# Modulation products on two column groups, second halves inside the recurrent heads, constants behind the first modulation weights

## What is computed

```python
def _modulation(cond, w_ada, b_ada):
    m = jnp.einsum('bd,de->be', jax.nn.silu(cond), w_ada) + b_ada
    return tuple(jnp.split(m[:, None, :], 6, axis=-1))

# in each layer
shift1, scale1, gate1, shift2, scale2, gate2 = mods
h = _rms(x, norm1_w) * (1 + scale1) + shift1
p = h @ w_in          # attention, recurrence (HGRN2, both directions), 2-D DFT, side by side
x = x + gate1 * (mix @ w_out)
h2 = _rms(x, norm2_w) * (1 + scale2) + shift2
x = x + gate2 * moe(h2)    # 4 groups of 4 experts, top-1 group, top-2 expert
```

## Time and profile before

| | |
|---|---|
| median of 3 runs | 1977.4 us (1970.61 to 1978.65) |
| the profiled execution | 1976.31 us; its span from first to last instruction 1974.5 us |
| PE busy, PEld busy | 1718.8 us (87%), 1199.9 us (61%) |
| DVE, ACT, POOL busy | 684.0 us (35%), 432.1 us (22%), 317.5 us (16%) |
| mean granted TensorE clock | 0.929 |
| L1331, modulation products | 768 records, 178.1 us |
| HBM traffic | 279.46 MB read, 34.60 MB written |

### The profile page before, as it was taken

How to read it: one execution, slowest core, us unless ns; L and a number is a source line. 1 busy time by engine, 2 the same in 40 slices (tenths; PEclk the granted TensorE clock), 3 DMA queues, 4 the chain that set the end, 5 groups by cost and what they waited for, 6 DMA issues and landing times.

```text
span 1974.5 us, 24830 instructions
## 1 busy us (share of the span) xinstructions
PE 1718.8 (87%) x10290; PEld 1199.9 (61%) x10290; DVE 684.0 (35%) x1200; ACT 432.1 (22%) x750; POOL 317.5 (16%) x303
## 2 busy tenths in 40 slices
PE   5899998776798999999998989887669968999993
PEld 2345556565654568888844555566565547888873
DVE  1107523577401312122114672356760151212223
ACT  1413232522102210000014313353220121000002
POOL 4000003854100010000010000276320001000001
PEclk9999997978699899999999989898789969999996
DMA  9672111000001489999995211000000038999975
GB/s 326 202 249 65 43 51 37 1 2 2 1 28 58 160 295 356 369 361 368 344 359 188 45 54 51 24 2 2 1 3 0 0 158 291 368 366 365 362 263 170
DMA packets 143495, 315.67 MB, mean 160 GB/s; under 512 B 25024, under 2 KB 99192, under 8 KB 130456
## 3 DMA queue, kind: packets, MB, share of 16 engines
q1 hardware_dynamic: 120240, 241.88, 36.1%
q0 software_dynamic: 11104, 37.26, 5.1%
q10 hardware_dynamic: 12040, 34.95, 4.5%
HBM read 279.46 MB, written 34.60 MB: 159 GB/s over the span
## 4 chain that ended last, share of the span: by engine, by line
PE 77%; DVE 11%; ACT 6%; issue 3%; DMA 2%; SPq 0%; ACTq 0%; POOL 0%; DVEq 0%; POOLq 0%
PE ps L1289 18%; PE ps L1660 18%; PE ps L1674 9%; PE ps L1331 8%; ACT scr L550 4%; PE ps L1401 3%; PE ps L1514 3%; PE ps L1644 2%; PE ps L1424 2%; PE ps L1439 2%; DVE scr L914 2%; PE ps L1318 1%; PE ps L1569 1%; DVE hT L1085 1%; DMA ring<-in_w_ada_dram 1%
## 5 line engine op out<-in xcount | busy, mean ns | idle before, releaser
L1660 PEld LDWEIGHTS ps<-hT,ring 128*128 128x128 f32 x3200 | 366.2, 193 | 26.4 <-issue 22.0
L1660 PE MATMUL ps<-hT,ring 128*128 128x128 f32 x3200 | 367.0, 276 | 3.4 <-ACT hT L550 3.4
L1289 PE MATMUL ps<-hT,ring 128*128 128x512 f32 x960 | 269.6, 442 | 18.2 <-DVE pT L959 12.7
L1289 PEld LDWEIGHTS ps<-hT,ring 128*128 128x128 f32 x960 | 149.7, 195 | 140.4 <-issue 127.1
L1331 PE MATMUL ps<-ring,cond 128*2 128x256 f32 x768 | 178.1, 387 | 11.6 <-DMA ring<-in_w_ada_dram 7.0
L550 ACT ACTIVATE pT<-ps 128x256 f32<-128x256 f32 (+3 forms) x74 | 33.5, 458 | 677.4 <-PE ps L1660 488.3
L1674 PE MATMUL ps<-ring,pT 128*128 128x512 f32 x400 | 179.6, 592 | 0.0
L517 POOL DMA_INDIRECT pT<-h_rows,slot_tok x50 | 47.2, 944 | 796.0 <-PE ps L1644 427.7
L478 POOL TENSOR_SCALAR scr<-scr,st 128x640 f32<-128x640 f32 (+1 forms) x80 | 129.1, 1627 | 73.8 <-DVE st L968 73.8
L1289 PE MATMUL ps<-pT,ring 128*128 128x512 f32 (+1 forms) x512 | 139.0, 434 | 1.7 <-ACT pT L550 1.7
L1249 DVE TENSOR_TENSOR pT<-ps,pT 128x256 f32<-128x256 f32 x50 | 21.2, 424 | 324.5 <-ACT pT L550 324.5
(11 more groups left out here) (212 smaller groups left out, 1961.1 us busy)
## 6 DMA issues: line engine op xcount, KB each, us to landing
ring<-in_w_gate_dram SPq DMA_DIRECT2D x50, 1024.0 KB, 7.4
ring<-in_w_up_dram SPq DMA_DIRECT2D x50, 1024.0 KB, 7.7
ring<-in_w_down_dram SPq DMA_DIRECT2D x50, 1024.0 KB, 6.9
ring<-in_w_ada_dram SPq DMA_DIRECT2D x48, 1024.0 KB, 6.3
y_rows<-pT ACTq DMA_DIRECT2D x50, 512.0 KB, 8.1
ring<-in_w_in_dram SPq DMA_DIRECT2D x14, 1024.0 KB, 5.3
h_rows<-scr ACTq DMA_DIRECT2D x10, 512.0 KB, 2.6
ring<-in_w_in_dram SPq DMA_DIRECT2D x16, 256.0 KB, 4.6
```

The costliest lines, as they stand in the source:

```text
L1289: ins = mm(out[:, a:b], lhs, rhs[:, a:b], start=start, stop=stop, **kw)
L1660: last = mm(bank(2 + j, P, at + c * P), w[:, k, c * P:(c + 1) * P], xk[:, j, k, :], start=(k == 0), stop=(k == KC - 1))
```

## The change

Five things, one after the other:

- A product writes to two column groups: even k to rows 0 to 31 of the bank, odd k to rows 32 to 63, with 32 stationary columns each (`cond` becomes a flat row of 46, so that columns 2k and 2k+1 are the wanted ones and the other 30 are other k's or zeros). ScalarE copies 64 rows, and a matmul with a 64 x 2 selector `sel` adds the two groups and turns the row into columns, in place of the transpose.
- The second half of each layer moves into that layer's recurrent heads: in the two units with d = 0, six items each, one ahead of the diagonal and one behind each of the first five levels. Their rows go to bank 7 beside the output products, one buffer, and their columns to another place of bank 7. The list of weights has them between the projection and the output weights of the layer.
- `norm` on ScalarE is split in `root` and `shift`. In layer 0 PE does the norm sums first, then the 12 items, and ScalarE the root first.
- SP loads only `ident` and `ones` ahead of x. Nine constants follow the issue of the second projection item ("MID"), `dft_s` and `dft_p` the fifth ("LATE"); the waits move to the first users. The cast of `lvl` follows the scaling of layer 0's norm on VectorE, and ScalarE waits for it before its first projection evacuation.
- The combine of layer 0 has no modulation items; `weigh` runs straight on.

```diff
@@ weight_stream
         if l == 0:
-            s += [("ada", l, i) for i in range(2 * ADA_HALF)]
+            s += [("ada", l, i) for i in range(ADA_HALF)]
         s += [("in", l, i) for i in range(IN_ITEMS)]
+        s += [("ada", l, ADA_HALF + i) for i in range(ADA_HALF)]
         s += [("out", l, i) for i in range(OUT_ITEMS)]
         if l + 1 < DEPTH:
             s += [("ada", l + 1, i) for i in range(ADA_HALF)]
         s += expert_items(l)
-        if l + 1 < DEPTH:
-            s += [("ada", l + 1, ADA_HALF + i) for i in range(ADA_HALF)]
@@
-CONSTS = ("ident", "blockones", "ones", "rot", "tri", "dft64", "cosT", "sinT",
-          "dft_s", "dft_p", "lvl", "restart", "tileno")
+CONSTS = ("ident", "ones", "restart", "lvl", "blockones", "rot", "cosT", "sinT", "tri", "dft64", "tileno",
+          "dft_s", "dft_p")
+FIRST_CONSTS, MID_CONSTS, LATE_CONSTS = CONSTS[0:2], CONSTS[2:11], CONSTS[11:]
@@ rows of a product
+        def ada_row(i):
+            return bank(2 + i % 2, 256)
+        def ada_row_next(i):
+            return bank(4 + i % 2, 256)
+        ada_row_heads = bank(7, 256, P)
+        HEADS_MODS = 3 * P
@@ sync
+                if (kind, l, i) == ("in", 0, 1):
+                    for c in MID_CONSTS:
+                        sp.dma_start(lvl_f if c == "lvl" else K[c][:], C[c]).then_inc(consts_in, 16)
+                if (kind, l, i) == ("in", 0, 4):
+                    for c in LATE_CONSTS:
+                        sp.dma_start(K[c][:], C[c]).then_inc(dft_in, 16)
@@ scalar
             act.wait_ge(zero_done, 3)
-            ada(0, 0)
             for l in range(DEPTH):
+                root(l, 0)
+                if l == 0:
+                    for i in range(ADA_HALF):
+                        ada(0, 0, i, ada_row(i))
                 act.wait_ge(mods_ok, 2 * l + 1)
-                norm(l, 0)
+                shift(l, 0)
                 if l == 0:
-                    ada(0, 1)
+                    act.wait_ge(lvl_ok, 1)
@@
                             A_(scr[:, 2 + i % 2, :], scr[:, 2 + i % 2, :], ACT.Exp).then_inc(lv_e, 1)
+                            if d == 0 and i >= 1:
+                                ada(l, 1, 6 * p + i - 1, ada_row_heads)
+                        if d == 0:
+                            ada(l, 1, 6 * p + 5, ada_row_heads)
@@ vector
+            seq(V.memset(cond[:], 0.0))
+            V.tensor_tensor(sel[:], ident[0:64, 0:2], ident[0:64, 32:34], ALU.add)
...
-            dve.wait_ge(consts_in, 16 * N_CONST)
-            seq(V.tensor_copy(K["lvl"][:], lvl_f))
@@
                 norm(l, 0)
                 if l == 0:
-                    modulations(0, 1)
+                    dve.wait_ge(consts_in, 16 * N_CONST)
+                    V.tensor_copy(K["lvl"][:], lvl_f).then_inc(lvl_ok, 1)
@@
+                modulations(l, 1)
                 dve.wait_ge(f_ab, l + 1)
@@ tensor
+            def ada_product(l, half, i, row, evacuated):
+                w = item(ITEM["ada", l, ADA_HALF * half + i]).rearrange("p (k n) -> p k n", k=KC)
+                if evacuated > 0:
+                    pe.wait_ge(ada_sb, evacuated)
+                for k in range(KC):
+                    r = slice(32 * (k % 2), 32 * (k % 2) + 32)
+                    last = mm(row[r, :], cond[:, 2 * k:2 * k + 32], w[:, k, :], start=(k < 2), stop=(k >= KC - 2))
+                last.then_inc(ada_ps, 1)
+            def ada_columns(l, half, i):
+                pe.wait_ge(ada_sb, (2 * l + half) * ADA_HALF + i + 1)
+                for j in range(2):
+                    last = mm(bank(7, 2, HEADS_MODS * half + 4 * i + 2 * j), mrow[:, i % 2, j * P:(j + 1) * P], sel[:],
+                              start=True, stop=True)
+                last.then_inc(ada_tr, 1)
@@
-            ada(0, 0, 0, ADA_HALF)
-            pe.wait_ge(consts_in, 16 * N_CONST)
-            pe.wait_ge(late_in, 16 * 16 * DEPTH)
             for l in range(DEPTH):
                 norm(l, 0)
                 if l == 0:
-                    pe.wait_ge(mods_ok, 1)
-                    pe.wait_ge(nrs, 1)
-                    ada(0, 1, 0, ADA_HALF)
+                    ada(0, ada_row, 0, ADA_HALF)
@@ in the heads, after the state products
+                        def row_product(a):
+                            ada_product(l, 1, 6 * p + a, ada_row_heads, (2 * l + 1) * ADA_HALF + 6 * p + a)
+                        if d == 0:
+                            row_product(0)
@@ in the heads, after each level's scores
                             last.then_inc(g_ps, 1)
+                            if d == 0 and i <= 5:
+                                ada_columns(l, 1, 6 * p + i)
+                                if i < 5:
+                                    row_product(i + 1)
@@ in the combine
-                if l + 1 < DEPTH:
-                    pe.wait_ge(dn_sb, MT * (l + 1))
-                    ada(l + 1, 1, 0, ADA_AT[0])
```

More of the change, by code:

```diff
@@ L377, in _ @@
         def _(sp):
-            sp.dma_start(K["ident"][:], C["ident"]).then_inc(x_in, 16)
+            for n in FIRST_CONSTS:
+                sp.dma_start(K[n][:], C[n]).then_inc(x_in, 16)
             sp.dma_start(xrow[:, 0, :], A["x_prompt"][0]).then_inc(x_in, 16)
             sp.dma_start(xrow[:, 1:TT, :], A["x_sample"][0].rearrange("(t p) d -> p t d", p=P)).then_inc(x_in, 16)
-            for n in CONSTS[1:]:
-                sp.dma_start(lvl_f if n == "lvl" else K[n][:], C[n]).then_inc(consts_in, 16)
             def next_item(n):
@@ L584, in _, with root @@
                     A_(xT[:, :, t * P:(t + 1) * P], ps[:, 0:1024].rearrange("p (k t) -> p k t", k=KC), ACT.Copy).then_inc(xt_act, 1)
-            def norm(l, which):
+            def root(l, which):
                 n0 = (l * 2 + which) * KC
@@ L600, in norm, with shift @@
                 A_(rs, rs, ACT.Exp, scale=-0.5).then_inc(nrs, 1)
+            def shift(l, which):
+                n0 = (l * 2 + which) * KC
                 for k in range(KC):
@@ L605, in norm, with ada @@
                            bias=mods[:, l, 3 * which, k, g:g + 1]).then_inc(h_ok, 1)
[L607 to L614, removed]
+            def ada(l, half, i, row):
+                n = (2 * l + half) * ADA_HALF + i
+                act.wait_ge(ada_ps, n + 1)
+                if n >= 2:
+                    act.wait_ge(ada_tr, n - 1)
+                A_(mrow[:, i % 2, :], row[0:64, :], ACT.Copy).then_inc(ada_sb, 1)
             def evacuated(l, u):
@@ L739, in _ @@
                     A_(pT[:, C_FT + p, 0:NP], bank(7, NP), ACT.Copy).then_inc(f_os, 1)
-                norm(l, 1)
+                root(l, 1)
+                shift(l, 1)
                 act.wait_ge(lgt_ps, l + 1)
@@ L756, in _ @@
                 if l + 1 < DEPTH:
-                    ada(l + 1, 0, 0, 5)
+                    for i in range(5):
+                        ada(l + 1, 0, i, ada_row_next(i))
                 act.wait_ge(rt_m, 2 * l + 1)
@@ L762, in _ @@
                 if l + 1 < DEPTH:
-                    ada(l + 1, 0, 5)
+                    for i in range(5, ADA_HALF):
+                        ada(l + 1, 0, i, ada_row_next(i))
                 def half_x(i):
@@ L882, in modulations @@
                 seq(V.tensor_tensor(mods[:, l, 3 * half:3 * half + 3].rearrange("p s k g -> p (s k) g"),
-                                    bank(7, 48).rearrange("p (n g) -> p n g", g=2), bias, ALU.add))
+                                    bank(7, 48, HEADS_MODS * half).rearrange("p (n g) -> p n g", g=2), bias, ALU.add))
                 at = (PA_N1, PA_N2)[half] + 8 * l
@@ L1271, in _ @@
                                                ALU.mult, ALU.add).then_inc(x_new, 1)
-                if l + 1 < DEPTH:
-                    modulations(l + 1, 1)
         @block.tensor
@@ L1319, in norm, with ada @@
                     mm(bank(6, NP), ones[:], sq[:, 0:NP], start=(k == 0), stop=(k == KC - 1)).then_inc(nsum, 1)
-            def ada(l, half, first, end):
+            def ada_product(l, half, i, row, evacuated):
[12 more added lines that the diff above has]
+                last.then_inc(ada_tr, 1)
+            def ada(l, row, first, end):
                 for i in range(first, end + (end == ADA_HALF)):
-                    n = (2 * l + half) * ADA_HALF + i
                     if i < ADA_HALF:
-                        w = item(ITEM["ada", l, ADA_HALF * half + i]).rearrange("p (k n) -> p k n", k=KC)
-                        if n >= 2:
-                            pe.wait_ge(ada_sb, n - 1)
-                        for k in range(KC):
-                            last = mm(bank(4 + i % 2, 256)[0:2, :], cond[:, :, k], w[:, k, :], start=(k == 0), stop=(k == KC - 1))
-                        last.then_inc(ada_ps, 1)
-                    if i >= 1:
-                        pe.wait_ge(ada_sb, n)
-                        for j in range(2):
-                            last = nc.tensor.transpose(bank(7, 2, 4 * (i - 1) + 2 * j), mrow[:, (i - 1) % 2, j * P:(j + 1) * P],
```

(5 more changed lines are left out.)

38 lines of the change are left out of this document (17 added, 21 removed).

## The result

The changed kernel takes 1919.8 us (1919.5 to 1921.4), the kernel before 1977.3 (1970.6 to 1978.7). The ratio is 0.9717, with a 95% interval of 0.9695 to 0.974: 57.5 us faster, where 54.5 were forecast. The profiled execution took 1921.4 us, with a span of 1919.6.

What follows compares the result with a forecast made beforehand. It took TensorE's program order to bound the first 138 us. Gains of 72.5 (start), 13 (routing) and 9 (combine) less 40 (heads) gave 54.5 us: 1976.3 to 1921.8, stated as a median of 1923 us, range 1900 to 1950.

Steps and rivals of the forecast that it cites:

- The product: Modulation product on two column groups: 1.9 us in place of 3.55, with a 0.45 us merge 2.35 an item against 3.76.
- The start: Up to layer 0's first projection: norm ahead of products and shorter items gain 72.5 us, bounds 66 to 76.
- Weights that land earlier: At the start, with constants moved back, the first weights land near 18 us instead of 30.0.
- The wait for lvl: Before ScalarE's first projection evacuation: lvl copy and its wait cost nothing; seeing that wait on ScalarE would be wrong.
- The heads: Six second-half items in each of four d=0 units: 11 us a unit, 40 us in all, bounds 28 and 56.
- each d=1 unit: In the recurrent heads: each d=1 unit following a d=0 unit starts warm and takes 1 us less.
- The routing: Layer 0's routing, with twelve first-half products of layer 1 at 2.35 for 3.76 us: 13 us gained, 8 to 17.
- The combine: End of layer 0, without layer 1's second-half products: 9 us gained, 6 to 11, after 1.9 to 4 for lower clock.
- (a): Rival on the products: the pairs don't overlap and stay at 3.55 us; 26 us slower, 2002 us; chance 7%.
- (b): Rival on the heads: clock stays at 0.50 through d=0 units, 35 us more a unit; 2022 us; chance 3%.
- (d): Rival on the heads: clock stays at 1.00 between units, 6 us a unit; 1903 us; chance 12%.
- (c): Rival on the products: half of the pairing is lost, 2.6 us a product; 1950 to 1965 us; chance 9%.

## Why the prediction was right, and where it was not

**The product** was forecast at 1.9 us with a merge of 0.45, 2.35 an item; the pitch is 2.38. The row that carried it halves the pitch of records of 128 columns; the products' 16 records at 256 columns take 1.85 / 16 = 116 ns each against 3.57 / 16 = 223 in one group, and 63 in four. The merge is 0.53 between products and 0.34 between score groups, on both sides of the 0.45. The Trainium skill (TensorE: Matmul & The Clock Gate, Part 3: Packing small matmuls) says that weight loads overlap matmuls in flight only where the row group differs. By that rule an estimated 0.4 us a product were at stake; the runs here don't agree for column groups: 1.85 us against the 1.78 of an exact half leaves 0.07.

**The start** was forecast at -72.5 and came at -69.5. The mechanism was right, item by item: the wait is the norm, the last item's transfer is late next, and from the last product's end to the projection it takes 68.66 - 64.82 = 3.8 us where 1.6 + 2.2 were worked out. Two terms were mis-sized. The norm's last sum was placed at 33.9 and ended at 35.96: its first sums run at the lower clock, which the prediction put into 1.5 us for the whole start. And from the first product's end to the last landing it takes 62.9 - 37.8 = 25.1 us where 5.3 + 6 x 3.0 = 23.3 were worked out. Weights that land earlier were a step of the argument, and the run with the constants first shows that it carries nothing: the norm covers it. The wait for lvl, named as a sign of being wrong, is not there: its cast ends at 75.4 and the first evacuation starts at 80.6, behind TensorE.

**The heads** were forecast at +40 and cost 36.8 by the two kernels with and without the second halves (18.4 a layer), 33.6 by the profiles of before and after. The latter is less because the last unit of layer 0 took 34.6 us with its tail in the profile of before, against 28.2 in the kernel without the second halves and 27.4 and 29.3 in two runs of the changed kernel, so that profile has some 6 us in it which are no property of the change. A unit was put at 31.5 us (its terms add up to 31.3) and takes 29.3 and 30.5. Of the 2.2 us in the first unit, 1.1 are the clock (put at 2.8 us; the state products' 2.50 for 1.35 and the first product's 2.42 for 1.85 make 1.7, as the clock rises inside the first product), and five levels at 3.51 in place of 3.65 are 0.7, the merge's 0.34. From the last level's merge to the output products 5.5 us were worked out and 369.91 - 364.43 = 5.5 are there. What failed is a small step: each d=1 unit was to be 1 us shorter for its warm start. In the changed kernel the d=1 units take 20.0 and 18.9 us, without the second halves 18.9 and 20.0: one is longer, the other shorter, and the gain isn't there. That TensorE takes VectorE's place as the bound of a level was right: 3.51 us against 2.53.

**The routing** was forecast at -13 and came at -9.0 in this profile, -11.5 in the second run of the same kernel. The chain of waits of the changed kernel there:

```profile
598.21 4.88 DMA h_rows<-scr
...
606.22 5.69 PE ps L1350 x32
...
637.80 3.54 PE ps L1350 x16
...
641.87 1.85 PE ps L1350 x16
```

The same write of h_rows took 2.58 us in the kernel before and 2.62 without the second halves. It takes 4.88 us in the kernel with the pairing alone too and 4.14 with four groups, and the former has no items in the heads, so it does not take them to lengthen it; what does was not tested. TensorE comes out of that wait at the lower clock: two products in 5.69 us, and another in 3.54 behind VectorE's slot arithmetic. The second run has 4.50, 4.51 and 1.85 in these places. Neither the 2.3 us of the write nor more than 1 us of clock stood in the sum: in the kernel before the three products beside the slot arithmetic lasted longer than it (686.2 to 699.0), and now TensorE is busy 8.7 of its 11.1 us.

**The combine** was forecast at -9 and came at -9.6: from the gather to the squares 34.9 us where 34.7 were worked out, and the norm's sums at the lower clock (985.53 to 996.4 against 9.0 us before) give back 1.9 where 1.9 to 4 were allowed.

**Not in the sum**: attention in layer 0 became 3.6 us shorter, with TensorE's granted clock at 0.95 on the mean (its two levels are 1.2 and 2.4 GHz) where it was 0.88 (layer 1: 0.93 in both, 96.4 and 96.3 us), and the experts 2.1 us longer. The rows of the changed kernel for attention in both layers (busy time of PE, PEld, DVE, ACT, POOL, then PEclk, DMA share, GB/s):

```profile
245.00:341.00 96.00, 69.84 (x657) 50.36 (x659) 53.28 (x129) 46.07 (x121) 71.31 (x48) 0.95 0.04 13
...
1190.00:1286.00 96.00, 69.98 (x653) 50.06 (x651) 53.10 (x128) 46.02 (x121) 70.93 (x48) 0.93 0.04 13
```

In the stretch of before TensorE was busy 74.1 of 99.0 us for the same instructions. Why the clock is higher there was not followed up. The other kernels have 94.8 to 98.2 us in this stage, and the second run of the changed kernel has 294.7 in the experts where the first has 297.8, so neither can be put down to the change. So the total of 54.9 by the profiles against 54.5 is in part luck: start 3.0 short, routing 4.0 short, heads 6.4 better (3.2 by the better comparison), the combine 0.6 better, and what was not in the sum 0.4 better together.

**The rivals**: (a) was built as a kernel and came out at 2005, where 2002 was worked out: its price was right, its condition isn't met. (b) fell: the clock rises with the first product. (d), cheaper heads, is what happened by a third: 9.3 us a unit in place of 11 or 6. (c) was not met either.

## What to carry to other kernels

Matmuls with few stationary columns can share the array: split the sum over k on column groups, add the rows in a matmul that had to be there anyway, and see whether four groups do better than two. When an instruction that fills an engine's gaps becomes half as long, look at what those gaps were covering: here an evacuation queued behind sixteen other ScalarE instructions, a ring that stood full, and a clock that falls in the gap each took a part back in one of the kernels. A ring of transfers stands still while its first consumer waits for something else; put the first consumers where the other work has its own gaps.

## What was not expected of the hardware

- Four column groups run at once: 16 records of 256 columns in 1.00 us (63 ns each), against 1.85 in two groups and 3.57 in one.
- The same four records of a merge take 0.34 us between instructions of their own form and 0.53 to 0.54 between others, with 64 rows or 128.
- The wait of TensorE for small loads on ScalarE's queue ended at 18.6 us in one kernel and between 14.2 and 16.0 in the others, two of them with the same bulk constants queued ahead; what sets it is open.
- A product behind idle time takes 3.23 and 3.54 us in two groups and 1.94 in four, against 1.85 and 1.00. The product after it can be back at 1.85, but in the routing of the kernel with the pairing alone three in a row took 3.50 to 3.56, and with four groups four in a row took 1.87.
